# Start addresses of the matrix-multiply operands: multiples of 256 bytes in place of multiples of 32

## What is computed

```python
for l in range(2):                                   # encoder
    h = h + 0.5 * swiglu_ffn(rms_norm(h, g1), w_in1, w_out1)      # 1024 -> 2 x 2816 -> 1024
    h = h + hybrid_mixer(rms_norm(h, g2), ...)       # stick-breaking heads and gated delta heads
    h = h + memory_cross_attention(rms_norm(h, g3), rms_norm(mem, g4), ...)
    h = h + 0.5 * swiglu_ffn(rms_norm(h, g5), w_in2, w_out2)
h = rms_norm(h, final)
for l in range(2):                                   # decoder
    proj = rms_norm(h, g) @ w_in                     # heads, gates, z
    h = h + (sum of gate * (branch_out * silu(z)) @ w_up) @ w_out
```

## The kernel before

| operand | start | start mod 256 |
|---|---|---|
| ring, w_lo | 1152 | 128 |
| w_hi | 42112 | 128 |
| const, h | 66688, 78400 | 128, 64 |
| xs (with xn) | 86592 | 64 |
| sq, rstd, mrstd, ssum | 102976 and after | 64 |
| arena, a, mg | 120544 | 224 |
| ob, xo | 136928, 145120 | 224 |
| yx | 169920 | 192 |
| wab, ms | 211072, 211584 | 128 |

## Time and profile before

### The profile page before, as it was taken

The page is one execution under the profiler, slowest core; times in us unless marked ns, Lnnn a source line. Parts: engine busy times, 40 slices in busy tenths (PEclk is TensorE's granted clock), DMA queues, the critical chain, the costliest instruction groups (busy, mean ns, idle before and its releaser), DMA issues.

```text
span 1870.8 us, 35544 instructions
## 1 busy us (share of the span) xinstructions
PE 1836.3 (98%) x15226; PEld 1740.2 (93%) x15226; DVE 1221.6 (65%) x1876; ACT 959.9 (51%) x1475; POOL 67.9 (4%) x32
## 2 busy tenths in 40 slices
PE   7999999999999999999999999999999999999999
PEld 7999998889999999999988899999988989988889
DVE  6775576764766567755767647665774578763676
ACT  6544467255544455444673555444653565653562
POOL 0000011400000000000114000000000000000000
PEclk9999999999999999999999999999999999999999
DMA  8555543333555655555433335555545335446332
GB/s 330 192 192 183 178 140 110 104 123 122 183 188 185 205 187 183 190 182 173 144 113 103 125 114 180 190 184 184 163 156 195 129 110 170 164 147 218 125 111 93
DMA packets 84460, 302.39 MB, mean 162 GB/s; under 512 B 9168, under 2 KB 11728, under 8 KB 84176
## 3 DMA queue, kind: packets, MB, share of 16 engines
q1 hardware_dynamic: 84304, 300.13, 48.2%
HBM read 299.04 MB, written 1.05 MB: 160 GB/s over the span
## 4 chain that ended last, share of the span: by engine, by line
PE 92%; DVE 5%; ACT 2%; issue 1%; DMA 0%; SPq 0%; DVEq 0%; ACTq 0%
PE bank L395 23%; PE bank L398 22%; PE bank L399 22%; PE bank L701 2%; DVE w_lo L1564 2%; PE bank L930 1%; PE bank L417 1%; PE bank L416 1%; PE bank L413 1%; PE bank L460 1%; PE bank L628 1%; PE bank L1015 1%; PE bank L464 1%; PE bank L465 1%; PE bank L1066 1%; PE bank L903 1%
## 5 line engine op out<-in xcount | busy, mean ns | idle before, releaser
L1564 DVE TENSOR_TENSOR w_lo<-ring,w_hi 128x1024 fp32r<-128x1024 f32 x544 | 660.4, 1247 | 114.5 <-ACT w_hi L1133 113.5
L1133 ACT ACTIVATE w_hi<-ring 128x1024 fp32r<-128x1024 f32 x544 | 563.5, 1053 | 282.2 <-PE bank L395 223.7
L395 PE MATMUL bank<-xs,w_hi 128*128 128x256 f32 x2448 | 693.2, 283 | 0.0
L399 PE MATMUL bank<-xs,w_lo 128*128 128x256 f32 x2448 | 683.8, 279 | 0.0
L398 PE MATMUL bank<-xs,w_hi 128*128 128x256 f32 x2448 | 683.6, 279 | 0.0
L395 PEld LDWEIGHTS bank<-xs,w_hi 128*128 128x128 f32 x2448 | 464.4, 190 | 4.9 <-issue 3.8
L398 PEld LDWEIGHTS bank<-xs,w_hi 128*128 128x128 f32 x2448 | 461.5, 189 | 3.1 <-issue 2.9
L399 PEld LDWEIGHTS bank<-xs,w_lo 128*128 128x128 f32 x2448 | 462.6, 189 | 0.0
L398 PE MATMUL bank<-a,w_hi 128*128 128x256 f32 x704 | 199.0, 283 | 0.0
L395 PE MATMUL bank<-a,w_hi 128*128 128x256 f32 x704 | 198.7, 282 | 0.0
L399 PE MATMUL bank<-a,w_lo 128*128 128x256 f32 x704 | 197.7, 281 | 0.0
(11 more groups left out here) (393 smaller groups left out, 3047.6 us busy)
## 6 DMA issues: line engine op xcount, KB each, us to landing
ring<-in_w SPq DMA_DIRECT2D x560, 512.0 KB, 3.3
arena<-in_mem SPq DMA_DIRECT2D x2, 1024.0 KB, 12.8
const<-in_const SPq DMA_DIRECT2D x1, 1395.0 KB, 15.9
h<-in_x SPq DMA_DIRECT2D x1, 768.0 KB, 7.8
out<-h SPq DMA_DIRECT2D x3, 256.0 KB, 2.5
dec_par<-in_dec SPq DMA_DIRECT2D x1, 615.0 KB, 19.6
h<-in_x SPq DMA_DIRECT2D x1, 256.0 KB, 4.2
out<-h SPq DMA_DIRECT2D x2, 128.0 KB, 2.0
```

What stands on the lines that cost most here:

```text
L395: last = nc.tensor.matmul(o, wh, hi(x, k0 + k), start=k == 0, stop=False, skip_group_check=True)
L399: last = nc.tensor.matmul(o, wl, hi(x, k0 + k), start=False, stop=k == nk - 1, skip_group_check=True)
L1133: nc.scalar.activation(w_hi[:, s * UNIT:(s + 1) * UNIT], ring[:, u % RU, :], AF.Copy).then_inc(sems("w_hi"), 1)
L1564: nc.vector.tensor_tensor(w_lo[:, r * UNIT:(r + 1) * UNIT], ring[:, r, :], w_hi[:, s * UNIT:(s + 1) * UNIT].bitcast(F32), ALU.subtract).th ...
```

## The change

`here` takes a name and rounds up to 256. Where the next multiple of 32 isn't one of 256, it allocates a padding tensor for the bytes between. `parts` moves its start in the arena to the next multiple of 64 floats. The arena's room is taken after the padding. The two lines around `ob` let its end lie beyond the bytes it shares. No instruction is added, removed or moved, and nothing but addresses changes.

```diff
-        def here():
-            return -(-nc.sbuf_base // 32) * 32
+        def here(name):
+
+            at_ = -(-nc.sbuf_base // 32) * 32
+            if at_ % 256:
+                sb(f"{name}_pad", -at_ % 256 // 4)
+            return -(-at_ // 256) * 256
...
-        ring_at = here()
+        ring_at = here("ring")
         ring = sb("ring", RU, UNIT)
         w_lo = rounded("w_lo", RU * UNIT, ring_at)
-        hi_at = here()
+        hi_at = here("w_hi")
         sb("w_hi_room", HU, UNIT)
         w_hi = rounded("w_hi", HU * UNIT, hi_at)
         const = sb("const", CONST.n)
         h = sb("h", KD, T)
-        xs_at = here()
+        xs_at = here("xs")
...
+        arena_at = here("arena")
         room = (nc.sbuf_bytes_remaining // 4 // 8) * 8 - 64
-        arena_at = here()
         arena = sb("arena", room)
...
         def parts(name, k):
 
-            n0 = at[0]
+            n0 = at[0] = -(-at[0] // 64) * 64
             return take(k, 2, T), rounded(name, k * 2 * T, arena_at + 4 * n0)
...
         obf, ob = parts("ob", 8)
-        assert at[0] == after_pairs
+        at[0] = max(at[0], after_pairs)
```

## The result

The changed kernel took **1906.01 us**, the median of four runs (1904.67 to 1908.73), against 1874.84 (1872.01 to 1877.09) for the kernel before: ratio 1.0165, 95% interval 1.0144 to 1.0185. It is slower by 31 us, where 17 us faster was forecast. The rival "the two streams meet" had 1909.

What follows compares the result with a forecast made beforehand. TensorE was taken as the bound: number of matmuls times distance between starts. Gains on a, ob, mg, xo, ms and yx sum to 16.3 us: 1874.7 − 16.3 = 1858 us, own range 1848 to 1868, full range 1828 to 1910.

Steps and rivals of the forecast that it cites:

- the two streams meet: fp32r matmuls: moving start relative to weights counts; equal remainders keep 120 ns, xs loses 36 us, 1909; chance 0.27.
- What bounds the kernel: Whole kernel: TensorE, busy 98% of the span, fed on time; time is number of matmuls times distance between starts.
- The zeros for ScalarE and VectorE: Operations of ScalarE and VectorE get other addresses; priced at 0 us, means staying 1053 and 1247 ns.
- the price of the unseen case: fp32r products with both operands at remainder 0: taken as 115.5 ns a matmul, the middle of xs's levels.
- the two ends: Bounds from the rows for both operands at remainder 0: 113.3 ns from below, 120.0 from above.
- The table of starts: Starts by 256 beside matmul distances: xs 64, 113.3 or 117.7; yx 192, 117.9; a, mg, ob, xo 224, 119.9; ms 128, 120.0.
- The slower rival: Same as "the two streams meet": xs slows to 120 ns, 36 us more, 1909; chance 0.27.
- Its sign that decides: Feed-forward input stretches: 835 matmuls in 100 us, no xs stretch near 113.3 ns, ms unchanged.
- The deeper floor: Aligned operands also lose 5.3 ns between 113.3 and 108 on some 12000 matmuls: 64 us beyond the first rival.
- The first rival: All fp32r products reach 113.3 ns if partly filled 256-byte lines cost the rest: 38.7 us less, 1834; chance 0.22.
- Nothing: Rival: levels come by chance or from something other than the start; 1875, give or take 5; chance 0.18.
- The rule of 16-byte lines: SBUF has 16-byte cachelines, penalty only for crossing; remainders 224 and 64 equally good, sum 0 and not 16 us.

Runs made afterwards that it cites:

- the four kernels of starts: TensorE alone, computation left out, 72-matmul streams: 28 start pairs; 26 differences; 36 w_hi/w_lo pairs; fewer weight columns. Lowest settled level 113.3 ns.
- the first kernel of starts: TensorE alone, computation left out: 28 pairs of weights and moving starts, four streams each; 120.0 ns at difference 0, 113.3 or 117.8 at −64.

## Why the prediction was wrong

**What bounds the kernel** was read rightly: matmuls times the distance of their starts; the distance made 34.7 of the 36.5 us of busy time. The zeros for ScalarE and VectorE held (1053 and 1248 ns, against 1053 and 1247), as did that for the DMAs (0% of the chain that ended last, before and after).

**The step that failed** is the price of the unseen case: "I take neither end but what xs shows now, since it is the tensor with the most matmuls and it starts at a multiple of 64, as all will: the middle of its levels, 115.5 ns." It measured 119.9, so the steps came to 34.7 us more where the sum had 16.3 less. The reason given for the choice, the absolute start, isn't what the distance depends on. What the two ends allowed was right, and the upper one, that of ms, was the answer. Term by term: `a` 0 and not −9.3 us; ob, mg and xo 0 and not −4.6; ms 0 and not −1.7; yx +0.8 and not −0.7; xs +33.3 and not 0; the weights moving 512 columns against xs 227.6 ns a step before and 228.0 after for w_hi, 231.7 and 227.3 for w_lo, which over 126 and 62 steps is 0.2 us less, and so 0 within its ±1.

**The table of starts had the answer.** I read its right column as it stood, called 224 slow because it isn't a multiple of 64, and put ms aside as an exception. With the weights' 128 taken from each entry there is no exception: 96 and 0 are slow, 64 is in the middle, −64 has two levels. The column needed one subtraction.

**The slower rival** was right in mechanism as far as it went (the relative start), place (every stretch of xs) and price: 36 us and 1909, against 33.3 us from xs and 1906. Its sign that decides, 835 matmuls in 100 us and ms unchanged, is what the windows show. The objection to it, that one tensor "is thin evidence", held my own reading to a lesser standard: that one had ms against it and nothing that explained the two levels. Its picture of the weight load that collides while it lasts isn't shown: a shorter load didn't shrink the spread.

**L424** was taken as a sign that "the cost is in the moving stream at full rate even where the weight load is small". With 32 columns the spread of 113.3 to 120.0 stays too, but other differences have the high price; that the moving stream has it by itself doesn't follow. The deeper floor below 113.3 ns isn't seen either: no stream of the four kernels of starts settled lower.

**The first rival**, all at the fast level, 1834, had the right floor: the kernel that reaches it took 1838. Its condition, whole lines of 256 bytes, was wrong; whole lines at equal starts are the slow case. **Nothing** was wrong too, though it was right that both levels of xs come without any change of address. The wide range, 1828 to 1910, takes 1906 in only because it was stretched over the slower rival; the forecast's own was 1848 to 1868.

The rule of 16-byte lines (the Trainium skill, SBUF — State Buffer, Door 1: The DMA port swizzle) would have made all starts in the kernels here equal, and by their differences they are up to 6.7 ns a matmul apart (113.3 and 120.0). The same page of the Trainium skill, section Who interferes with whom, gives PE two read ports, one for the moving operand and one for the weight load, and calls them independent. No run here looks at ports. If it is taken to mean that the two operands' starts don't bear on each other in time, the measurements don't agree: 1906 and 1838 us come from the same instructions with only the relative starts changed.

## What to carry to other kernels

Where TensorE bounds and reloads weights for every matmul, tabulate moving start minus stationary start, modulo 256, for each product, and compare stretches by that; aligning everything to the same boundary gives all of them difference 0, here among the slowest at 120.0 ns. Treat weights that alternate in a fixed pattern as one case and measure the pattern with TensorE alone in several streams, then confirm the best one in the kernel: 64 bytes one way for w_hi and the other way for w_lo were worth 2% here. A table from stretches with one exception is a sign to look for another variable before pricing a change by it.

## What the runs showed of the hardware

- Distance between the starts of fp32r matmuls with 256 moving and 128 stationary columns at the upper clock: 120.0 ns at difference 0 and 96, 117.8 or 113.3 at 64 and −64, 115.6 at −8. For the 27 pairs tried with a difference that is a multiple of 32 it depends on the difference modulo 256 and not on either start, and it is the same with no DMA of weights under way as at a DMA share of 0.6.
- Two levels for one and the same instruction stream. The level settles some six matmuls after a break and lasts, through up to 1,584 matmuls, until the next break or a new difference; with difference −64 it was 113.3 ns in 15 of 20 streams of the first kernel of starts. How the stream is entered seems to bear on it: behind a break of 40 or 104 columns difference −64 was fast in all 16 streams of the four kernels of starts (128 columns of weights, A = B), behind 8 or 200 columns in 9 of 16. No run varied the break by itself, so what chooses the level is open. The 10 us between the two kernels at −64 (weights moved, or activations moved) are put down to it from one trace of each.
- The pattern settles as a whole: w_hi at difference 0 with w_lo at 64 gives 117.8 ns for every step, −64 with 64 gives 113.3, and 64 with −64 gives 118.9.
- With 64 stationary columns difference 0 gives 113.3 ns and −64 gives 119.0, the other way round than with 128. With 128, 96, 64 and 32 columns the values tried span 113.3 to 120.0 alike.
